# Buffers, order and slots of a two-block transformer kernel: six weight buffers, four row buffers, two late output units

## The chip, the cores and the metric

The kernel runs on one core of a Trainium2 chip. The metric is the device time of one execution in microseconds; the time before is 3179.68 us, the median of three runs (3179.25 to 3179.78).

## The reference

The input x has 256 tokens of width 2048, all in float32. A first block mixes and then applies retrieved experts; a second block has two layers. What matters here:

```python
# first block: attention (MLA and Fox heads, gated), then experts
x = x + jnp.einsum('bse,ed->bsd', merged, w_out[layer])
h2 = rms_norm(x, ffn_norm_g[layer])
...
# experts of one token: 8 heads, 16 experts each, out of 128 x 128
s1, i1 = lax.top_k(scores[:, :, 0], PEER_TOPK)
s2, i2 = lax.top_k(scores[:, :, 1], PEER_TOPK)
top_scores, top_pos = lax.top_k(cand_scores, PEER_TOPK)
experts = jnp.take_along_axis(cand_idx, top_pos, axis=-1)
...
a = jnp.einsum('td,thkd->thk', xb, u[eb])          # 128 rows of u for each token
w = gates * jax.nn.gelu(a, approximate=False)
x = x + jnp.einsum('thk,thkd->td', w, v[eb])       # 128 rows of v for each token
# second block, twice:
proj = x @ w_in
y = jnp.concatenate([ya, yb, yc], axis=-1) @ w_out # attentions and a convolution
x = layer_norm(ALPHA * x + y, ln_g, ln_b)
```

## The kernel before

The tokens are two tiles t = 0, 1 of 128, one token to a partition. There are eight passes in this order (PASSES): layer1(0), experts(0), layer1(1), experts(1), then layer2(l, t) as (0, 0), (1, 0), (0, 1), (1, 1). In layer 2 the run number is r = 2t + l + 1, so the last two passes are r = 3 and r = 4; tile 1 needs keys and values of tile 0 only.

Weights. All weight matrices are cut into units of 128 x 2048 floats, 1 MB. STREAM lists the units of all passes in the order in which PE uses them; each is 4 matmuls of 128x512, shown in the trace as 8 instructions. SP goes through FETCHES and loads them into a ring of RING = 4 slots; it waits until PE has used the unit that had the slot. Some units go two by two in one transfer of 2 MB (PAIRED, from a given row of a pass on), which needs both slots free. On PE, `unit()` waits for the arrival. `units` (L1445) multiplies with the normalised input, `out_units` (L1481) and `fin_units` (L1489) sum the output product in the four banks of psO; the last four units of a pass, "fin", each finish one bank.

Expert rows. For each tile POOL gathers 128 rows of u and 128 of v for every token: one `gather(n)` (L1001) brings one row of 2048 floats to each of 128 partitions, 1 MB, n = 0 to 511. They land in NB = 6 buffers `rows` and, in some ranges of n, one more in `hrow`. `allowed(n)` says which buffers a gather may use: the last one holds the work space of the top-k selection of tile 0 until that is over. DVE takes row after row in `slot()`: a dot product (L398) for u, a multiply-add into x (L405) for v. `row_used` lets POOL reuse the buffer.

Who does what when is written out by hand. `stage(m)` gives DVE m rows to work through during a stage, and `mix(f)` makes it go up to the fraction f of them at that place; EMIX, MIX1 and MIX2 hold the numbers. So DVE's rows for tile 0 lie in experts(0), layer1(1) and experts(1), those for tile 1 in experts(1), layer2(0, 0) and layer2(1, 0). SP starts to fetch for layer2(0, 1) when all but four rows are used, and that pass begins when all are.

The selection in `experts(t)`: for each i of four, two heads, PE computes queries (units), transposes them (`keys_T`) and multiplies with the sub-keys (`scores`, L1758). DVE copies the scores (L749), takes the 16 best twice (`top16`) and writes expert numbers to `eid`; `ids_ready` then lets POOL gather. In the order before, PE has one unit of the next chunk ahead of keys_T and one ahead of scores.

In layer 2, r = 2 leaves its sums in psO; DVE takes them at the start of r = 3 (`add_out(0, 0.0)`, L567), and with ACT's squares (`layer_squares`) makes the statistics (`layer_end`); `apply_ln(0)` in r = 3 writes the result of tile 0, and POOL stores it between its two convolutions. Between r = 3 and r = 4, layer_end gives the normalised x of tile 1 (L948, `xh_ready`), which PE transposes in `x_first` (L1457).

The fetch loop and the rule for pairs:

```python
_two = _u % 2 == 0 and _u + 1 < len(STREAM) and STREAM[_u][0] in PAIRED and STREAM[_u + 1][0] == STREAM[_u][0] \
    and STREAM[_u][1] >= PAIRED[STREAM[_u][0]] and STREAM[_u][2] == STREAM[_u + 1][2] == UNIT
...
if (p, row) == (("b", 0, 1), 0):
    sp.wait_ge(row_used, 4 * SLOTS - 4)
```

## Time and profile before

| | |
|---|---|
| median of three runs | 3179.68 us |
| the profiled execution: its time, its span | 3179.64 us, 3177.5 us |
| PE busy | 2525.9 us, 79% |
| DVE busy | 1922.3 us, 60% |
| POOL busy | 1059.2 us, 33% |
| ACT busy | 532.5 us, 17% |
| DMA | 1193.54 MB, mean 376 GB/s |
| SP's queue (weights); POOL's queue (gathers) | 644.12 MB; 538.86 MB |
| chain that ended last | PE 41%, DMA 39%, DVE 9%, POOL 6% |
| mean granted TensorE clock | 0.898 of full |

PE's sequence of busy tenths in 40 slices begins with seven nines, falls to 5 to 8 in the middle, and ends with nines again; the DMA's is nine in nearly all slices. Times in the trace are microseconds from the start of the span. A row with [2.23 <-DMA ring<-in_w] says that the engine was idle 2.23 us before it and what released it. The queue of SP is SPq, and a row of it covers several issues merged. "PE psP" and the like name the tile that is written.

### The profile page before, as it was taken

The page shows a single profiled execution, that of the slowest core. Times are in us where ns is not written, and L with a number is a line of the kernel's source. Part 1 is how long each engine was busy: PE and PEld are TensorE (multiplying, and loading weights), DVE is VectorE, ACT ScalarE, POOL GpSimd, SP SyncE. Part 2 cuts the span into 40 slices and gives each one's busy share as a digit, 9 for nine tenths or more (in the row PEclk, how much of TensorE's full clock was granted, in tenths as well). Part 3 has the DMA queues.
Part 4 walks back from the last instruction along what each step waited for, and adds up shares of the span by engine and source line. Part 5 has one row for each costly group of instructions (what it writes and reads, how often), then busy time and mean ns, then how long its engine had stood idle before and what let it go on. Part 6 is the DMA issues. An engine that isn't in the chain of part 4 may idle for free.

```text
span 3177.5 us, 20533 instructions
## 1 busy us (share of the span) xinstructions
PE 2525.9 (79%) x6976; PEld 1226.4 (39%) x6976; DVE 1922.3 (60%) x2978; ACT 532.5 (17%) x1371; POOL 1059.2 (33%) x649
## 2 busy tenths in 40 slices
PE   9999999837667668585879676566886589999998
PEld 4444444413233234233435332222543234444443
DVE  1656544877576666666895656675676653452533
ACT  3222122111102101011104201011410011111111
POOL 0000000355363444543443445533553424400710
PEclk9999999968879878787999888788898799999999
DMA  9888888999999999999999999999999999988886
GB/s 341 293 305 293 291 288 304 421 421 424 424 420 424 424 417 425 423 416 420 418 424 394 423 424 424 423 421 424 424 421 425 423 369 323 314 303 269 282 290 230
DMA packets 152280, 1193.54 MB, mean 376 GB/s; under 512 B 16552, under 2 KB 20280, under 8 KB 23536
## 3 DMA queue, kind: packets, MB, share of 16 engines
q1 hardware_dynamic: 73184, 644.12, 53.8%
q0 software_dynamic: 74192, 538.86, 40.8%
q10 hardware_dynamic: 4800, 9.25, 0.8%
q8 instruction: 56, 0.92, 0.1%
q14 instruction: 48, 0.39, 0.0%
HBM read 1190.07 MB, written 2.10 MB: 375 GB/s over the span
## 4 chain that ended last, share of the span: by engine, by line
PE 41%; DMA 39%; DVE 9%; POOL 6%; issue 3%; ACT 1%; DVEq 0%; SPq 0%; ACTq 0%
PE psP L1445 29%; DMA rows<-in_peer_u,tk 16%; DMA rows<-in_peer_v,tk 15%; PE psO L1481 6%; POOL rows L1001 5%; DMA ring<-in_w 4%; DVE rows L398 3%; DMA hrow<-in_peer_v,tk 2%; DVE x_sb L405 2%; PE psO L1489 2%; DMA ring<-in_wq 1%; DMA hrow<-in_peer_u,tk 1%; PE psX L1557 1%; POOL hrow L1001 1%; PE psO L1803 1%
## 5 line engine op out<-in xcount | busy, mean ns | idle before, releaser
L1445 PE MATMUL psP<-ring,hT 128*128 128x512 f32 x3584 | 1661.6, 620 | 135.2 <-DMA ring<-in_w 125.9
L1445 PEld LDWEIGHTS psP<-ring,hT 128*128 128x128 f32 x3584 | 700.5, 200 | 1010.4 <-issue 893.2
L1001 POOL DMA_INDIRECT rows<-in_peer_u,tk x222 | 391.8, 1765 | 981.1 <-DVEq L770 525.3
L405 DVE SCALAR_TENSOR_TENSOR x_sb<-rows,tk,x_sb 128x2048 f32<-128x2048 f32 x223 | 524.3, 2351 | 232.0 <-DMA rows<-in_peer_v,tk 214.5
L398 DVE CUSTOM_DVE_ANT_0 rows<-rows,hrow 128x2048 f32<-128x2048 f32 x222 | 503.5, 2290 | 214.0 <-DMA rows<-in_peer_u,tk 210.1
L1001 POOL DMA_INDIRECT rows<-in_peer_v,tk x223 | 394.2, 1768 | 471.7 <-DVE x_sb L405 392.6
L1481 PE MATMUL psO<-ring,work 128*128 128x512 f32 x832 | 390.0, 623 | 38.3 <-issue 22.8
L422 DVE STREAM_TRANSPOSE work<-work 32x128 f32<-32x128 f32 (+2 forms) x864 | 271.1, 314 | 151.0 <-ACT work L1321 83.2
L1481 PEld LDWEIGHTS psO<-ring,work 128*128 128x128 f32 x832 | 164.4, 202 | 236.0 <-issue 227.6
L1595 PE MATMUL psX<-kst,work 128*128 128x128 f32 x68 | 16.5, 388 | 157.5 <-DVEq L547 145.5
L1445 PE MATMUL psP<-ring,work 128*128 128x512 f32 (+1 forms) x288 | 122.4, 579 | 24.0 <-DMA ring<-in_w 23.5
L1134 ACT ACTIVATE work<-work,small 128x256 f32<-128x256 f32 (+1 forms) x128 | 56.6, 443 | 424.3 <-DVEq L519 424.3
L405 DVE SCALAR_TENSOR_TENSOR x_sb<-hrow,tk,x_sb 128x2048 f32<-128x2048 f32 x33 | 77.6, 2351 | 44.9 <-DMA hrow<-in_peer_v,tk 42.3
L398 DVE CUSTOM_DVE_ANT_0 hrow<-hrow 128x2048 f32<-128x2048 f32 x34 | 77.8, 2290 | 42.2 <-DMA hrow<-in_peer_u,tk 41.5
L1001 POOL DMA_INDIRECT hrow<-in_peer_u,tk x34 | 65.9, 1939 | 101.3 <-DVE tk L398 78.6
L1489 PE MATMUL psO<-ring,work 128*128 128x512 f32 x192 | 89.1, 622 | 11.5 <-DMA ring<-in_w 10.1
L1445 PEld LDWEIGHTS psP<-ring,work 128*128 128x128 f32 x288 | 57.3, 202 | 85.0 <-issue 82.5
L1001 POOL DMA_INDIRECT hrow<-in_peer_v,tk x33 | 58.9, 1785 | 89.1 <-DVE x_sb L405 72.5
L1303 ACT ACTIVATE work<-kst,cols 128x128 f32<-128x128 f32 x248 | 76.1, 389 | 46.1 <-PE psO L1803 46.0
L1020 POOL TENSOR_TENSOR work<-work 128x512 f32<-128x512 f32 x60 | 76.2, 1271 | 4.7
L1595 PEld LDWEIGHTS psX<-kst,work 128*128 128x128 f32 x68 | 10.9, 194 | 169.7 <-DVEq L547 155.4
L1803 PE MATMUL psO<-work 128*128 128x128 f32 x496 | 63.7, 283 | 15.0 <-ACT work L1303 15.0
(368 smaller groups left out, 1649.6 us busy)
## 6 DMA issues: line engine op xcount, KB each, us to landing
ring<-in_w SPq DMA_DIRECT2D x332, 1024.0 KB, 5.4
ring<-in_w SPq DMA_DIRECT2D x120, 2048.0 KB, 11.6
ring<-in_wq SPq DMA_DIRECT2D x32, 1024.0 KB, 9.4
ring<-in_w SPq DMA_DIRECT2D x8, 512.0 KB, 5.9
rows<-in_peer_v,tk POOLq DMA_INDIRECT x223, 22.5
rows<-in_peer_u,tk POOLq DMA_INDIRECT x222, 21.1
rows<-in_gate_bias SPq DMA_DIRECT2D x1, 2048.0 KB, 12.5
work<-in_sub_keys ACTq DMA_DIRECT2D x2, 1024.0 KB, 8.0
```

The costliest lines, as they stand in the source:

```text
L398: V.tensor_tensor_reduce(out=row_buf(n), in0=row_buf(n), in1=hrow[:, t, :], scale=1.0, scalar=0.0, op0=ALU.mult, op1=ALU.add, accum_out=do ...
L405: V.scalar_tensor_tensor(out=x_sb[:, t, :], in0=row_buf(n), scalar=dots[t][:, k:k + 1], in1=x_sb[:, t, :], op0=ALU.mult, op1=ALU.add).then ...
L422: own.add(V.transpose(dst[b_:b_ + 32, :, a_:a_ + 32], src[a_:a_ + 32, :, b_:b_ + 32]))
L1001: pool.indirect_dma_start(out=row_buf(n), out_offset=None, in_=a["peer_u" if s < SLOTS else "peer_v"], in_offset=bass.IndirectOffsetOnAxis ...
L1020: own.link(T(cacc, cacc, csq, ALU.add))
L1134: ins = A(W4[:, j, :], W4[:, j, :], ACT.Exp, bias=negm[:, 4 * u + j:4 * u + j + 1], accum_out=lsum[:, 4 * u + j:4 * u + j + 1])
L1303: ins = A(diag[n % 2][:, c, :], ident, ACT.Copy, scale=col("conv_w", (l * CC + c) * TAPS + k))
L1445: last = MM(psP[:, c % 2, 0:wide], src[:, kk, :], w[:, k, :], start=(kk == 0 and not begun), stop=(kk == 4 * nu - 1))
L1481: last = MM(psO[:, d, :], src[:, k, :], w[:, d, :], start=(bool(first) and k == 0), stop=False)
L1489: last = MM(psO[:, d, :], src[:, k, :], w[:, k, :], start=False, stop=(k == 3))
L1557: last = MM(o, qT[:, j, :], kT[:, j, :], start=plain, stop=(plain or bank_ends))
L1803: last = MM(psO[:, 0, P * m:P * (m + 1)], diag[n % 2][:, m, :], convh[:, m, k:k + P], start=(k == 0 and m == 0), stop=(k == TAPS - 1 and m ...
```

## The change

- The ring has six slots instead of four; `rows` four buffers instead of six. The one further buffer in hrow stays. The last of the four is open from n = 16 (4 + the 12 rows planned in experts(0)) instead of the last of six from n = 15.
- experts(0): PE transposes the first queries and computes their scores before it goes on to the next chunk. DVE's selection is the function `choose(t, i, h0, h1)` for heads h0 to h1; for the first two heads it runs head by head, and after the first one `head_ready` opens gathers 0 to 15; gather 16 waits for the second head.
- Pairs: all units of layer1(1), layer2(0, 0) and layer2(1, 0) that make a pair in the packed weights go two by two, instead of from row 24 or 8 on.
- The rows in experts(0) are 0, 1, 3, 5, 3 in its five stages instead of 0, 0, 4, 5, 0, and 11 instead of 14 in the first stage of layer1(1). The fractions of layer2(0, 0) change from 0.35, 0.45, 0.6 to 0.6, 0.65, 0.8.
- Late units: of the four last units of layer2(1, 0) the third and fourth move behind layer2(0, 1). PE multiplies them (`late_unit`) at the start of layer2(1, 1), one before the first transposes of x and one after the second, into banks of psO that are free by then, from a copy of the left operand kept in `mT_late`. DVE takes the incomplete sums at the start of r = 3 (`take_sums`), and adds the late part and makes the statistics in r = 4 (`add_late`, then layer_end). ACT's squares and apply_ln of tile 0 move to r = 4 too, and POOL stores tile 0 after both convolutions. The order of the statistics semaphores becomes TURN.

Left out of the diff: the two new semaphores' names in the lists, context lines, and the old selection, which is the same as choose for both heads.

```diff
@@ -24,7 +24,7 @@
...
 UNIT = 2048
-RING = 4
+RING = 6
 NEG = -1.0e30
...
@@ -34,7 +34,7 @@
...
 SLOTS = PH * TOPK
-NB = 6
+NB = 4
 N1 = 8
...
@@ -61,16 +61,19 @@
...
-EMIX = [[0, 0, 4, 5, 0], [10, 6, 6, 6, 0]]
-MIX1 = [14, 28, 21, 35, 21, 34, 20, 33, 25]
+EMIX = [[0, 1, 3, 5, 3], [10, 6, 6, 6, 0]]
+FIRST = TOPK
+MIX1 = [11, 28, 21, 35, 21, 34, 20, 33, 25]
 GELU1 = 4
 EARLY = 0.25
+LATE = 2
+TURN = {1: 1, 3: 2, 2: 3, 4: 4}
 MIX2 = [[20, 33, 63], [43, 32, 53]]
...
-    return list(range(NB - 1)) + ([NB - 1] if n >= 15 else []) + ([NB] if 24 <= n < 228 or n >= 256 else [])
+    return list(range(NB - 1)) + ([NB - 1] if n >= NB + sum(EMIX[0]) else []) + ([NB] if 24 <= n < 228 or n >= 256 else [])
...
@@ -125,15 +128,21 @@
...
     for _row, (_name, _g, _q) in enumerate(_order):
+        if _p == ("b", 1, 0) and _name == "fin" and _q >= LATE:
+            continue
         _kind = GROUPS[_g] if _p[0] == "a" else "n"
...
         STREAM.append((_p, _row, width(_name), _how, _ended[_how]))
-
-
-PAIRED = {("a", 1): 24, ("b", 0, 0): 8, ("b", 1, 0): 8}
+    if _p == ("b", 0, 1):
+        for _d in range(LATE, 4):
+            _ended["bank"] += 1
+            STREAM.append((("b", 1, 0), len(_order) - 4 + _d, UNIT, "bank", _ended["bank"]))
+
+
+PAIRED = {("a", 1): 0, ("b", 0, 0): 0, ("b", 1, 0): 0}
 ODD = {_p: [_u for _u, _s in enumerate(STREAM) if _s[0] == _p][0] % 2 for _p in PAIRED}
...
@@ -141,7 +150,7 @@
...
     _two = _u % 2 == 0 and _u + 1 < len(STREAM) and STREAM[_u][0] in PAIRED and STREAM[_u + 1][0] == STREAM[_u][0] \
-        and STREAM[_u][1] >= PAIRED[STREAM[_u][0]] and STREAM[_u][2] == STREAM[_u + 1][2] == UNIT
+        and STREAM[_u][1] >= PAIRED[STREAM[_u][0]] and (STREAM[_u][1] + ODD[STREAM[_u][0]]) % 2 == 0 and STREAM[_u + 1][1] == STREAM[_u][1] + 1 and STREAM[_u][2] == STREAM[_u + 1][2] == UNIT
     FETCHES.append((_u, 2 if _two else 1))
...
@@ -283,6 +292,7 @@
...
         mTc = qT
+        mT_late = v3(wk(768, 1280), P)
         diag = [csq, cacc]
...
@@ -295,7 +305,7 @@
...
         lnc = v3(kv[:, 2048:2304], P)
-        lnc_far = v3(rows[:, 4, 0:256], P)
+        lnc_far = v3(hrow[:, 0, 0:256], P)
...
@@ -574,6 +584,28 @@
...
+            def take_sums():
+
+                for d in range(4):
+                    if d < LATE:
+                        seen["bank"] += 1
+                    dve.wait_ge(bank_done, seen["bank"])
+                    V.tensor_copy(x_sb[:, 0, 512 * d:512 * (d + 1)], psO[:, d, :]).then_inc(x_added, 1)
+
+            def add_late():
+
+                for d in range(LATE, 4):
+                    seen["bank"] += 1
+                    dve.wait_ge(bank_done, seen["bank"])
+                    xv = x_sb[:, 0, 512 * d:512 * (d + 1)]
+                    V.tensor_tensor(xv, xv, psO[:, d - LATE, :], ALU.add).then_inc(late_added, 1)
+                dve.wait_ge(late_added, 4 - LATE)
+                dve.wait_ge(x_added, 16)
+                link(V.tensor_reduce(msum, v3(x_sb[:, 0, :], 512), AX, ALU.add))
+                link(V.tensor_reduce(part3[:, 0:1], msum[:, 0:3], AX, ALU.add))
+                link(V.tensor_scalar(shift[:, 0:1], part3[:, 0:1], -1.0 / 1536, None, ALU.mult))
+                dve.sem_inc(ln_part, 1)
+
             def turn_P(t):
...
@@ -588,12 +620,12 @@
...
                 link(V.tensor_scalar(dev, dev, -1.0, 1e-5, ALU.mult, ALU.add))
-                dve.wait_ge(sq_done, r)
+                dve.wait_ge(sq_done, TURN[r])
                 link(V.scalar_tensor_tensor(out=bias, in0=ssl[:, 0:1], scalar=1.0 / D, in1=dev, op0=ALU.mult, op1=ALU.add))
...
             def layer_rs(t, r):
-                dve.wait_ge(sd_ready, r)
+                dve.wait_ge(sd_ready, TURN[r])
                 link(V.reciprocal(rsl[:, t:t + 1], vart[:, 2:3]))
...
@@ -742,31 +774,43 @@
...
                 idx3 = v3(idxu, TOPK)
+
+                def choose(t, i, h0, h1):
+
+                    m, heads, ways, picks = h1 - h0, slice(256 * h0, 256 * h1), slice(32 * h0, 32 * h1), slice(16 * h0, 16 * h1)
+                    top16([(sc[:, j, :], vals[:, j, :], idx3[:, j, :]) for j in range(2 * h0, 2 * h1)])
+                    own.add(V.tensor_copy(idxf[:, ways], idxu[:, ways]))
+                    v4_ = vals[:, 2 * h0:2 * h1, :].rearrange("p (h c) k -> p h c k", c=2)
+                    d4 = idxf[:, ways].rearrange("p (h c k) -> p h c k", c=2, k=TOPK)
+                    c4 = cand[:, heads].rearrange("p (h a b) -> p h a b", a=TOPK, b=TOPK)
+                    e4 = eq[:, heads].rearrange("p (h k j) -> p h k j", k=TOPK, j=TOPK)
+                    link(V.tensor_tensor(c4, v4_[:, :, 0, :].unsqueeze(3).to_broadcast([P, m, TOPK, TOPK]),
+                                         v4_[:, :, 1, :].unsqueeze(2).to_broadcast([P, m, TOPK, TOPK]), ALU.add))
+                    best = gates[t][:, 32 * i:32 * (i + 1)]
+                    top16([(cand[:, 256 * h:256 * (h + 1)], best[:, 16 * h:16 * (h + 1)], posu[:, 16 * h:16 * (h + 1)])
+                           for h in range(h0, h1)])
+                    for c, (op, amount) in enumerate(((ALU.logical_shift_right, 4), (ALU.bitwise_and, 15))):
+                        link(V.tensor_scalar(posh[:, picks], posu[:, picks], amount, None, op))
+                        link(V.tensor_copy(posx[:, picks], posh[:, picks]))
+                        link(V.tensor_tensor(v3(eq[:, heads], TOPK), rep(posx[:, picks], TOPK), over(iota, 16 * m), ALU.is_equal))
+                        link(V.tensor_tensor(e4, e4, d4[:, :, c, :].unsqueeze(2).to_broadcast([P, m, TOPK, TOPK]), ALU.mult))
+                        link(V.tensor_reduce((p0, p1)[c][:, picks], v3(eq[:, heads], TOPK), AX, ALU.add))
+                    link(V.scalar_tensor_tensor(out=posx[:, picks], in0=p0[:, picks], scalar=float(NK), in1=p1[:, picks],
+                                                op0=ALU.mult, op1=ALU.add))
+                    link(V.tensor_copy(eid[t][:, 32 * i + 16 * h0:32 * i + 16 * h1], posx[:, picks]))
+
                 for i in range(4):
...
                     dve.sem_inc(sc_taken, 1)
...
+                    if t == 0 and i == 0:
+                        choose(t, i, 0, 1)
+                        dve.sem_inc(head_ready, 1)
+                        choose(t, i, 1, 2)
+                    else:
+                        choose(t, i, 0, 2)
                     dve.sem_inc(ids_ready, 1)
...
@@ -814,20 +858,22 @@
...
                 stage(MIX2[l][0] if t == 0 else 0)
-                early, last = (EARLY, 0.35, 0.45, 0.6) if l == 0 else (0.3, 0.83, 0.87, 0.92), (1.0, 1.1)[l]
+                early, last = (EARLY, 0.6, 0.65, 0.8) if l == 0 else (0.3, 0.83, 0.87, 0.92), (1.0, 1.1)[l]
                 if l == 0:
...
                 if r == 3:
-                    add_out(0, 0.0)
-                    layer_end(1, 0, 2)
+                    take_sums()
                     link(V.tensor_scalar(x_sb[:, 1, :], x_sb[:, 1, :], ALPHA, None, ALU.mult))
...
                 if r == 4:
+                    dve.wait_ge(lnrow_in, 64)
                     link(V.scalar_tensor_tensor(out=x_sb[:, 1, :], in0=x_sb[:, 1, :], scalar=ALPHA, in1=ln_g0, op0=ALU.mult, op1=ALU.mult))
                     link(V.scalar_tensor_tensor(out=x_sb[:, 1, :], in0=ln_b0, scalar=ALPHA, in1=x_sb[:, 1, :], op0=ALU.mult, op1=ALU.add))
+                    add_late()
+                    layer_end(1, 0, 2)
                 mix(early[0])
...
@@ -914,7 +960,7 @@
...
                         mix(1.0)
-                if l == 0 and t == 1:
+                if l == 1 and t == 1:
                     apply_ln(0)
...
@@ -990,9 +1036,11 @@
...
                 k, b = s % SLOTS, BUF[n]
-                if s < SLOTS and s % 32 == 0:
+                if s < SLOTS and (s % 32 == 0 and n or n == FIRST):
                     pool.wait_ge(ids_ready, 4 * t + s // 32 + 1)
-                if n == 15:
+                if n == 0:
+                    pool.wait_ge(head_ready, 1)
+                if BUF[n] == NB - 1 and NB - 1 not in BUF[:n]:
                     pool.wait_ge(ids_ready, 4)
...
@@ -1031,9 +1079,8 @@
...
                     conv(l, 1, step)
-                if l == 0:
-                    pool.wait_ge(x_norm, 4)
-                    pool.dma_start(out[:, 0, :], x_sb[:, 0, :]).then_inc(out0_sem, 16)
+            pool.wait_ge(x_norm, 4)
+            pool.dma_start(out[:, 0, :], x_sb[:, 0, :]).then_inc(out0_sem, 16)
             pool.wait_ge(out0_sem, 16)
...
@@ -1306,7 +1353,7 @@
...
                 take_xT(split, "copy" if l == 0 else "ln")
-                if l == 0 and t == 1:
+                if l == 1 and t == 1:
                     layer_squares(0, 2)
...
@@ -1379,7 +1426,7 @@
...
                 if t == 0:
-                    take_mT(mTc)
+                    take_mT(mT_late if l else mTc)
                 if r != 2:
...
@@ -1390,13 +1437,16 @@
...
                 own.link(A(vart[:, 3:4], kc("one"), ACT.Sqrt))
-                act.wait_ge(ln_part, r)
+                act.wait_ge(ln_part, TURN[r])
+                if r == 2:
+                    act.wait_ge(late_added, 4 - LATE)
                 own.add(A(junk[:, 0:1536], x_sb[:, t, 0:1536], ACT.Square, bias=shift[:, t:t + 1], accum_out=ssl[:, 0:1]))
...
                 act.sem_inc(sq_done, 1)
-                act.wait_ge(x_added, 8 + 4 * r)
+                if r != 2:
+                    act.wait_ge(x_added, 8 + 4 * r)
                 own.link(A(junk[:, 1536:2048], x_sb[:, t, 1536:2048], ACT.Square, bias=shift[:, t:t + 1], accum_out=ssl[:, 1:2]))
-                act.wait_ge(var_ready, r)
+                act.wait_ge(var_ready, TURN[r])
                 A(vart[:, 2:3], ssl[:, 1:2], ACT.Sqrt, scale=1.0 / D, bias=vart[:, 0:1]).then_inc(sd_ready, 1)
...
@@ -1446,7 +1496,7 @@
...
-            def x_first(split, src, ready, key, between=None):
+            def x_first(split, src, ready, key, between=None, head=None, mid=None):
...
@@ -1460,8 +1510,12 @@
...
+                if head is not None:
+                    head()
                 turn(0)
                 turn(1)
+                if mid is not None:
+                    mid()
                 c = begin(key)
...
@@ -1471,19 +1525,27 @@
...
-            def out_units(k0, k1, src, first, last_group=False):
+            def out_units(k0, k1, src, first, ends=4):
...
                     for d in range(4):
-                        last = MM(psO[:, d, :], src[:, k, :], w[:, d, :], start=(bool(first) and k == 0), stop=False)
+                        last = MM(psO[:, d, :], src[:, k, :], w[:, d, :], start=(bool(first) and k == 0), stop=(k == 3 and d >= ends))
                     last.then_inc(unit_used, 1)
-            def fin_units(src):
+            def late_unit(d):
+
+                pe.wait_ge(x_added, 16 + d - LATE + 1)
+                w = v3(unit(), 512)
+                for k in range(4):
+                    last = MM(psO[:, d - LATE, :], mT_late[:, k, :], w[:, k, :], start=(k == 0), stop=(k == 3))
+                last.then_inc(bank_done, 1)
+
+            def fin_units(src, upto=4):
                 pe.wait_ge(mT_ready, n_["mT"])
-                for d in range(4):
+                for d in range(upto):
                     w = v3(unit(), 512)
...
@@ -1762,6 +1824,11 @@
...
                     c = begin(("e", t, "pq", i))
+                    if t == 0 and i == 1:
+                        keys_T(0)
+                        scores(0)
+                        units(c, 0, 4, 4, hT)
+                        continue
                     units(c, 0, 1, 4, hT)
...
@@ -1783,7 +1850,8 @@
...
                 else:
-                    x_first(split, x_sb[:, t, :], lambda r_: pe.wait_ge(xh_ready, 4 * t + r_ + 1), ("b", l, t, "u", 0))
+                    x_first(split, x_sb[:, t, :], lambda r_: pe.wait_ge(xh_ready, 4 * t + r_ + 1), ("b", l, t, "u", 0), None,
+                            (lambda: late_unit(LATE)) if t else None, (lambda: late_unit(LATE + 1)) if t else None)
...
@@ -1815,6 +1883,8 @@
...
                     pe.wait_ge(x_added, before)
+                    if r == 4:
+                        pe.wait_ge(late_added, 4 - LATE)
                     pe.wait_ge(sc_taken, 8)
...
@@ -1911,8 +1981,8 @@
...
                 e_move()
-                out_units(2, 4, mT, None)
-                fin_units(mTc)
+                out_units(2, 4, mT, None, LATE if r == 2 else 4)
+                fin_units(mT_late if r == 2 else mTc, LATE if r == 2 else 4)
...
```

## Rows read from the trace of the kernel before

**Rows 1.** Windows, whole span: us; busy us by engine (instructions); TensorE clock; DMA share; GB/s.
```profile
0.00:545.00 545.00, 535.21 (x1460) 255.49 (x1461) 273.47 (x897) 138.94 (x366) 5.58 (x12) 1.00 0.88 300
545.00:2590.00 2045.00, 1417.97 (x3998) 702.08 (x3997) 1406.71 (x1494) 309.43 (x830) 908.87 (x510) 0.85 1.01 421
2590.00:3178.00 588.00, 572.73 (x1520) 268.83 (x1520) 242.09 (x589) 84.14 (x175) 144.74 (x127) 0.98 0.84 287
```

**Rows 2.** Timeline, start, SP and PE: start, us, engine, line, op, count [idle before].
```profile
29.38 0.43 SPq L1064 DMA_DIRECT2D rows<-in_gate_bias  x1
31.97 41.53 SPq L1061 DMA_DIRECT2D ring<-in_w  x12
...
44.56 13.97 PE L1445 MATMUL psP<-ring,hT 128*128 128x512 f32 x32 [2.23 <-DMA ring<-in_w]
```

**Rows 3.** DMA issues from 100 to 500 us: count, KB each, median us to landing.
```profile
ring<-in_w SPq DMA_DIRECT2D x106, 1024.0 KB, 5.3
```

**Rows 4.** Timeline, first expert pass: PE scores, DVE's copy of them, POOL's first gather.
```profile
524.16 1.05 PE L1758 MATMUL psO<-work 128*128 128x128 f32 x8
...
525.33 0.69 DVE L749 COPY rows<-psO 128x512 f32<-128x512 f32 x1 [14.80 <-PE psO L1758]
...
542.63 1.04 POOL L1001 DMA_INDIRECT rows<-in_peer_u,tk  x1 [525.35 <-DVEq L770]
```

**Rows 5.** Windows just before and just after the first gather.
```profile
505.00:542.00 37.00, 37.00 (x108) 17.96 (x108) 19.58 (x70) 12.30 (x18) 0.00 (x0) 1.00 0.78 266
...
550.00:560.00 10.00, 10.00 (x34) 5.17 (x33) 9.25 (x28) 0.60 (x1) 0.00 (x0) 1.00 1.01 427
```

**Rows 6.** DMA issues from 545 to 2590 us; then POOL's issues in the timeline.
```profile
ring<-in_w SPq DMA_DIRECT2D x120, 2048.0 KB, 11.6
...
rows<-in_peer_u,tk POOLq DMA_INDIRECT x220, 21.3
...
647.49 0.94 POOL L1001 DMA_INDIRECT rows<-in_peer_u,tk  x1 [4.04 <-DVE tk L398]
...
655.87 3.03 POOL L1001 DMA_INDIRECT rows<-in_peer_u,tk  x1 [2.47 <-DVE tk L398]
```

**Rows 7.** The page's groups: DVE's dot product with one gathered row.
```profile
L398 DVE CUSTOM_DVE_ANT_0 rows<-rows,hrow 128x2048 f32<-128x2048 f32 x222 | 503.5, 2290 | 214.0 <-DMA rows<-in_peer_u,tk 210.1
```

**Rows 8.** Waits from 1660 to 1700 us (total, times, longest); a window there.
```profile
DVE kv L533 <- PE psX L1514: 20.6, 1, 20.6
...
1690.00:1710.00 20.00, 20.00 (x91) 12.71 (x90) 11.35 (x18) 10.48 (x40) 7.01 (x5) 0.95 0.80 307
```

**Rows 9.** Timeline, end of the middle stage: SP's fetches, last rows, last units.
```profile
2581.37 30.20 SPq L1061 DMA_DIRECT2D ring<-in_w  x7
2583.56 2.35 DVE L405 SCALAR_TENSOR_TENSOR x_sb<-rows,tk,x_sb 128x2048 f32<-128x2048 f32 x1 [1.34 <-DMA rows<-in_peer_v,tk]
2590.00 8.67 PE L1489 MATMUL psO<-ring,work 128*128 128x512 f32 x16 [5.28 <-DMA ring<-in_w]
2590.35 2.35 DVE L405 SCALAR_TENSOR_TENSOR x_sb<-rows,tk,x_sb 128x2048 f32<-128x2048 f32 x1 [4.43 <-DMA rows<-in_peer_v,tk]
2595.29 2.35 DVE L405 SCALAR_TENSOR_TENSOR x_sb<-rows,tk,x_sb 128x2048 f32<-128x2048 f32 x1 [2.60 <-DMA rows<-in_peer_v,tk]
2598.51 1.04 PE L1457 MATMUL psX<-kst,x_sb 128*128 128x128 f32 x8
```

**Rows 10.** Timeline of PE and one window at the start of the last pass.
```profile
2865.55 13.90 PE L1489 MATMUL psO<-ring,work 128*128 128x512 f32 x32
...
2882.59 1.42 PE L1457 MATMUL psX<-kst,x_sb 128*128 128x128 f32 x8 [3.15 <-DVE x_sb L948]
...
2885.77 5.75 PE L1445 MATMUL psP<-ring,hT 128*128 128x512 f32 x8
...
2880.00:2890.00 10.00, 6.52 (x17) 3.58 (x18) 4.46 (x16) 4.12 (x11) 0.00 (x0) 0.66 0.34 116
```

**Rows 11.** Timeline, DVE's first work after apply_ln in the third pass.
```profile
2838.39 1.13 DVE L544 SCALAR_TENSOR_TENSOR work<-psX,small,work 128x128 f32<-128x128 f32 x4 [11.11 <-PE psX L1585]
```

27 lines of the change are left out of this document (4 added, 23 removed).

## Prediction

> **What bounds the kernel now.** The windows come first, because the busy shares of the whole span mix three stages. Up to 545 us PE is busy 535.21 of 545 us at a granted clock of 1.00 while the DMA moves 300 GB/s; from 545 to 2590 us the DMA share is 1.01 and it moves 421 GB/s, and PE is busy only 1418 of 2045 us at 0.85; after 2590 PE is bound again, 572.73 of 588 us [rows 1]. So stage 1 ends when PE has done its units, stage 2 when its bytes have come in, and stage 3 when PE has done the rest. In stage 2 a wait of PE or DVE costs nothing as long as some transfer is queued. There only three things can move the end: bytes fetched before stage 2 begins, bytes taken out of it, and its rate. A unit or a gathered row is 1.05 MB, 2.5 us at 421 GB/s.
>
> The profiled execution took 3179.64 us (span 3177.5, 2.1 around it); the median of three is 3179.68. I count changes of the span and subtract them from 3179.7.
>
> **Six ring buffers at the start.** The first nine ring fetches are issued one by one as slots come free, then x (tile 1) and the gate bias, 3 MB together, and only at 31.97 the tenth unit; PE waits 2.23 us for it at 44.56 [rows 2]. With six slots the tenth fetch is issued two units earlier (7 us: 32 matmuls of 13.97 us are four units), with the same 3 MB ahead of it. Gain between 0 and 2.23; the DMA is nearly full from 10 to 40 us, but it has some room before that. I take the whole: **-2.2**.
>
> **Six ring buffers at the border of stages 1 and 2.** In stage 1 the DMA has 29% to spare, and a unit lands 5.3 us after its issue [rows 3], so that the ring is full ahead of PE. With two more slots two more units (2.1 MB) are in when stage 2 begins. All of them are needed before stage 2 ends, so the gain is 2 x 2.5 us: **-5.0** (bounds 0 and -5.0; 0 if the deeper ring only shifts the balance to the rows' cost, which is case B below).
>
> **First row numbers by one head.** Before, PE transposes the first queries after one unit of the next chunk and computes scores after another (the scores' matmuls run at 524.16); DVE takes them at 525.33 and POOL issues the first gather at 542.63 [rows 4]. The new order has no unit between, which saves about 4 us to the scores (two units are 7, less an estimated 3 for ACT's two copies, which PE now sees bare). From the copy to the gather are 17.3 us, 16.6 without the copy, for two heads; one head has half the instructions in the top-16 steps and half the width in the others, but the fixed part of each small one stays: I take 9.9. So the first gather goes out at about 532, 11 us earlier. Until then the DMA moves 266 GB/s (505 to 542), and just after it 427 [rows 5]; nearer the usual 300 of stage 1 the spare is about 125 GB/s, so 11 us bring 1.4 MB, **-3.3** (bounds: -1.5 if three row buffers fill too soon, -4.5 with 427 against 266). Three buffers are 3.1 MB, and at that spare rate they last the 11 us. The second head costs DVE some 3 us more in all; DVE isn't what stage 2 waits for. The row plan moves three rows ahead of the pass (12 instead of 9) and takes 3 out of its first stage, sum nil. In the 5-row burst after the third selection only three rows can be at hand; DVE waits some 8 us there, covered by the ring, which still owes PE units. If that cover is gone, it is 8 us of half-used DMA, 4 us.
>
> **Slots placed anew.** Row buffers become 4 plus one in hrow instead of 6 plus one; with the ring the sum in flight stays 11 MB. Gathers land 21.3 us after their issue [rows 6], mostly queueing. What a row buffer needs without queueing: a unit's 5.3 us as the nearest row for landing, 0.93 to 3.03 for the issue on POOL, and 2.29 on DVE [rows 3, 6, 7], so 8.5 to 10.6 us; five buffers at full rate take 5 x 2.5 = 12.5 us per turn. So five rows alone still keep the DMA full, with little to spare. From gather 228 to 255 hrow is closed, and four buffers have only 10 us per turn; there the ring must help. I charge **+2** for longer dry stretches (bounds 0 and case B).
>
> The Trainium skill, SBUF — State Buffer, "Who interferes with whom", says that GpSimd and DVE share a port pair, and that POOL is held back while certain DVE instructions run. It speaks against fewer row buffers. Without it the turn of a buffer would be the 8.5 us and the charge nil; with it every gather may slip by a DVE instruction, the turn is 10.6, and the charge is the +2. The trace agrees: 0.93 us for an issue with DVE idle, 3.03 with DVE in its row loop.
>
> **The dip at 1690.** In the first pass over tile 0 in layer 2's part, DVE waits 20.6 us for PE's keys, the row buffers are all full, and the ring of two pairs has one pair in flight: 307 GB/s from 1690 to 1710 [rows 8] against 421 over the stage. That is 2.3 MB, 5.4 us. Now three pairs leave two in flight while PE uses the third, and the mix fractions (0.35, 0.45, 0.6 become 0.6, 0.65, 0.8) put 5 more of the 20 rows ahead of that wait. Fewer row buffers act against it. I take 0.7 of it: **-3.8** (0 to -5.4).
>
> **All pairs in the middle part.** 24 + 8 + 8 units of these passes now come two by two. A pair lands in 11.6 us [rows 6]. That is 181 GB/s, no more than a half of the DMA, and the total rate of 421 is that of a stage with both kinds: **-0.5** (0 to -1).
>
> **Two late output units.** They leave stage 2: 2.1 MB, at most -5.0. But look at its end. At 2581.37 four rows are left and SP may fetch for the next pass; PE waits 5.28 us for the last pair, uses it to 2598.5, and the last row is added from 2595.29 [rows 9]. Both end together. The gate for SP (four rows left) is unchanged, and now up to six free slots are filled at once with first units of the next pass, which share the DMA with the last rows just as the last pair did. Only what of the pair had moved before the gate is gained, about one unit, **-2.5**; the rest is early bytes for a stage that doesn't need them. Bounds 0 and -5.0.
>
> The Trainium skill, DMA: Bandwidth & Descriptors, "Queues, rings and completion order", says that each DMA engine takes turns between its queues, a packet at a time. A pair has runs of 16 KB and single units and rows 8 KB, so by that rule the last rows, which now share with single units, would get a half instead of a third; over the 12 us of the pair that is 2 us more, and the term would be -4.5. The trace leans that way: 6.8 us between the additions of two rows while the last pair is in flight (2583.56, 2590.35) and 4.9 beside single units (2590.35, 2595.29).
>
> In stage 3 the two units go into the change from layer 0 to layer 1 of tile 1. There PE is idle 3.15 us for the normalised x, then again for ACT's copies, and its clock drops to 0.66 of full, so that the first unit (8 matmuls) takes 5.75 us [rows 10] instead of 3.5. From the end of the output product (2865.55 + 13.90 = 2879.5) to the end of that unit are 12.1 us. Afterwards: three units at 3.5 (13.90 for four) and transposes of 1.1 and 0.6, 12.1 to 12.6 us with the clock at full. So 7 us of matmuls cost **+0.3** (bounds -0.5 and +3.5, if the second of them isn't hidden).
>
> DVE gets add_late, the statistics and apply_ln of tile 0 in the last pass. The first lie before the u chunk's copy is needed, with the 14 us of PE's next chunk between (four units). apply_ln is eight instructions on a quarter of a row's width, by 2.29 us for a row 4.6 us and something for the start of each; it sits at the same place of the pass as before, where DVE is idle 11.11 us behind it [rows 11]. Behind the waits of ACT's squares stands only its u copy. The write of out, tile 0, follows the last convolution on POOL, some 80 us before the end, and hides. All **0**.
>
> **Sum.** -2.2 - 5.0 - 3.3 + 2.0 - 3.8 - 0.5 - 2.5 + 0.3 = -15.0: 3179.7 - 15.0 = **3164.7**.
>
> **The rivals.** (A) Only the head start counts: the deeper ring and the early gathers bring 8.3 us, the dip stays because five row buffers are full sooner, the end isn't sooner by the late units, the start doesn't gain; with +2 this is 3173.4. For it: the end of stage 2 is balanced, and gains on one side alone do nothing there.
>
> (B) Slower: five row buffers run dry. Whenever DVE is away from rows (eight selections of 17 us each, waits up to 20.6 us) the rows' queue is empty two buffers sooner; if ring and rows are both stopped by each other, the DMA stands. The end of stage 2 moves by 2045 us times the loss in rate, and the 15 us are gone once 421 becomes 418. A mean of 416 costs 24.6 us: 3189. Against it: buffers in all are as many as before, and PE's and DVE's waits in stage 2 are mostly for the DMA.
>
> (C) Every term at its best: -2.2 - 5.0 - 4.5 - 5.4 - 1 - 5 - 0.5 and no charge for five buffers is -23.6: 3156.
>
> **How the numbers follow.** Forecast 0.55, A 0.20, B 0.10, C 0.15. The range reaches from below C to between A and B: 3152 to 3181. A measurement of this kernel can tell about 0.2%, 6.4 us, from no change: under 3173.3 lie the forecast, C and half of A: faster 0.80; same 0.11; slower 0.09.
>
> **What will show it.** First gather near 532 us, and the DMA above 420 GB/s from there; no PE wait at 42 to 44 us; 1690 to 1710 above 380 GB/s; the middle windows at 421 or more; the last row near 2584; PE without a gap between the output product and layer 1, clock 1.00. The prediction is wrong if the middle rate falls below 419, if the last rows take more than the 16 us they take now from SP's gate on, or if the last pass of stage 3 has new PE waits.

## The result: slower, 3246.9 us

Median of five runs 3246.89 us (3243.76 to 3249.51) against 3179.78; the ratio is 1.0206, 95% interval 1.0195 to 1.0216. The forecast was 3164.7, the range ended at 3181. The profiled execution took 3244.26 us, its span 3242.5.

The windows of the kernel after, in the first two stretches of [rows 1]:

```profile
core 0: us, PE busy (x) PEld busy (x) DVE busy (x) ACT busy (x) POOL busy (x), PEclk, DMA share, GB/s
0.00:545.00 545.00, 535.23 (x1461) 255.28 (x1462) 279.90 (x920) 138.94 (x366) 7.42 (x14) 1.00 0.89 307
545.00:2590.00 2045.00, 1309.56 (x3916) 665.50 (x3914) 1353.80 (x1458) 307.38 (x826) 843.40 (x490) 0.81 0.98 405
```

Stage 1 moves 307 GB/s where it moved 300: 545 us x 7 GB/s = 3.8 MB more are in when stage 2 begins. Stage 2 moves 405 where it moved 421, which is 3.8% of 2045 us, 78 us. PE is busy 1310 us of it, not 1418, and DVE 1354, not 1407: both wait longer. The border of stages 2 and 3 has moved by 64 us, from 2598.51 [rows 9] to 2662.55, and stage 3 lasts 580.0 us after, 579.0 before. The whole loss lies in stage 2. The timeline at its end:

```profile
2648.73 20.88 SPq L1108 DMA_DIRECT2D ring<-in_w  x7
2660.08 2.35 DVE L415 SCALAR_TENSOR_TENSOR x_sb<-hrow,tk,x_sb 128x2048 f32<-128x2048 f32 x1 [2.62 <-DMA hrow<-in_peer_v,tk]
2662.55 2.56 PE L1507 MATMUL psX<-kst,x_sb 128*128 128x128 f32 x12 [4.57 <-DVEq L837]
```

The page's part 2, in 40 slices of 81 us, the kernel after (the DMA's share in tenths, then GB/s):

```profile
DMA  9888888999999999999998999999999999989886
GB/s 377 299 301 285 299 285 323 379 394 390 422 397 411 408 408 413 419 394 405 421 385 352 424 417 422 409 393 425 410 417 414 419 389 326 320 283 300 280 290 219
```

There is no one place: of the slices 8 to 32, which are stage 2, 14 move less than 412 GB/s, and they are spread over all of it. In windows of 5 us from 545 to 2590 (409 of them) the DMA share is under 0.90 in 25, before in 2. The mean share fell from 1.009 to 0.984 (2.5%, 51 us in which DMA engines stood), and the GB/s for a full share from 417 to 412 (1.3%, 26 us). Together these two are the 78 us, within rounding. The 3.8 MB of the head start and the 2.1 MB of the two late units are 14 us less to move at 421 GB/s, and 78 less 14 is the 64 us by which the border moved.

### The profile page after: what moved, and what is told of

It reads as the page before. It is cut to its first block, busy times and chain, and to the rows that moved or that the text cites. A ratio compares the mean times of both kernels' runs of the same rounds, so it can differ in the third digit from the quotient of the medians.

```text
span 3242.5 us, 20545 instructions
## 1 busy us (share of the span) xinstructions
PE 2450.5 (76%) x6976; PEld 1205.1 (37%) x6976; DVE 1926.6 (59%) x2991; ACT 531.3 (16%) x1370; POOL 1034.3 (32%) x649
## 4 chain that ended last, share of the span: by engine, by line
PE 38%; DMA 34%; DVE 16%; POOL 7%; issue 4%; ACT 1%; DVEq 0%; SPq 0%; ACTq 0%; POOLq 0%
PE psP L1495 26%; DMA rows<-in_peer_v,tk 13%; DMA rows<-in_peer_u,tk 12%; PE psO L1535 6%; POOL rows L1049 6%; DVE x_sb L415 4%; DMA hrow<-in_peer_v,tk 4%; DMA hrow<-in_peer_u,tk 4%; DVE rows L408 4%; PE psO L1551 1%; PE psO L1871 1%; POOL hrow L1049 1%; DVE hrow L408 1%; PE psX L1619 1%; DMA ring<-in_w 1%
## 5 line engine op out<-in xcount | busy, mean ns | idle before, releaser
L1495 PE MATMUL psP<-ring,hT 128*128 128x512 f32 x3584 | 1607.9, 605 | 4.7 <-DMA ring<-in_wq 2.3
L1495 PEld LDWEIGHTS psP<-ring,hT 128*128 128x128 f32 x3584 | 687.2, 195 | 839.4 <-issue 828.1
L1049 POOL DMA_INDIRECT rows<-in_peer_u,tk x209 | 350.6, 1678 | 1026.9 <-DVEq L810 511.7
L415 DVE SCALAR_TENSOR_TENSOR x_sb<-rows,tk,x_sb 128x2048 f32<-128x2048 f32 x210 | 493.7, 2351 | 268.5 <-DMA rows<-in_peer_v,tk 252.9
L408 DVE CUSTOM_DVE_ANT_0 rows<-rows,hrow 128x2048 f32<-128x2048 f32 x209 | 475.3, 2290 | 264.9 <-DMA rows<-in_peer_u,tk 261.2
L1049 POOL DMA_INDIRECT rows<-in_peer_v,tk x210 | 364.8, 1737 | 515.5 <-DVE x_sb L415 448.4
L1535 PE MATMUL psO<-ring,work 128*128 128x512 f32 x832 | 380.9, 612 | 32.7 <-issue 32.7
L408 DVE CUSTOM_DVE_ANT_0 hrow<-hrow 128x2048 f32<-128x2048 f32 x47 | 107.7, 2291 | 60.0 <-DMA hrow<-in_peer_u,tk 58.3
L415 DVE SCALAR_TENSOR_TENSOR x_sb<-hrow,tk,x_sb 128x2048 f32<-128x2048 f32 x46 | 108.2, 2352 | 52.9 <-DMA hrow<-in_peer_v,tk 48.8
L1049 POOL DMA_INDIRECT hrow<-in_peer_u,tk x47 | 85.6, 1822 | 109.8 <-DVE tk L408 101.2
L1049 POOL DMA_INDIRECT hrow<-in_peer_v,tk x46 | 85.0, 1847 | 93.9 <-DVE x_sb L415 76.5
L1495 PE MATMUL psP<-ring,work 128*128 128x512 f32 (+1 forms) x288 | 113.5, 545 | 0.4 <-ACT work L1290 0.4
L1551 PE MATMUL psO<-ring,work 128*128 128x512 f32 x176 | 79.2, 609 | 1.4 <-ACT work L1194 1.4
L1495 PEld LDWEIGHTS psP<-ring,work 128*128 128x128 f32 x288 | 54.0, 190 | 55.6 <-issue 53.1
```

Of the source, the lines that this page charges most:

```text
L408: V.tensor_tensor_reduce(out=row_buf(n), in0=row_buf(n), in1=hrow[:, t, :], scale=1.0, scalar=0.0, op0=ALU.mult, op1=ALU.add, accum_out=do ...
L415: V.scalar_tensor_tensor(out=x_sb[:, t, :], in0=row_buf(n), scalar=dots[t][:, k:k + 1], in1=x_sb[:, t, :], op0=ALU.mult, op1=ALU.add).then ...
L1049: pool.indirect_dma_start(out=row_buf(n), out_offset=None, in_=a["peer_u" if s < SLOTS else "peer_v"], in_offset=bass.IndirectOffsetOnAxis ...
L1495: last = MM(psP[:, c % 2, 0:wide], src[:, kk, :], w[:, k, :], start=(kk == 0 and not begun), stop=(kk == 4 * nu - 1))
L1535: last = MM(psO[:, d, :], src[:, k, :], w[:, d, :], start=(bool(first) and k == 0), stop=(k == 3 and d >= ends))
L1551: last = MM(psO[:, d, :], src[:, k, :], w[:, k, :], start=False, stop=(k == 3))
```

## Where the DMA stands, in the trace

The timeline of the kernel after from 1688 to 1728 us: SP's row, some of POOL and DVE, and PE's. The columns are start, duration, engine and line, and in brackets the idle time before and who ended it:

```profile
1688.68 0.33 SPq L1106 DMA_DIRECT2D ring<-in_w  x1
...
1698.35 0.94 POOL L1049 DMA_INDIRECT rows<-in_peer_u,tk  x1 [6.46 <-DVE tk L408]
1698.83 0.87 DVE L736 MAX8 kv<-kv 128x8 f32<-128x128 f32 x4
1714.79 0.18 DVE L800 CAST tk<-kv 128x32 uint32<-128x32 f32 x1
1715.80 2.29 DVE L408 CUSTOM_DVE_ANT_0 rows<-rows,hrow 128x2048 f32<-128x2048 f32 x1 [0.19 <-DVE tk L820]
1718.37 2.75 POOL L1049 DMA_INDIRECT rows<-in_peer_u,tk  x1 [19.08 <-DVE tk L408]
...
1727.61 1.12 PE L1948 MATMUL psX<-kst,work 128*128 128x128 f32 x4 [39.31 <-DVE work L879]
```

and the windows of the same stretch:

```profile
1700.00:1705.00 5.00, 0.00 (x0) 0.00 (x0) 4.83 (x29) 0.00 (x0) 0.00 (x0) 0.50 0.99 415
1705.00:1710.00 5.00, 0.00 (x0) 0.00 (x0) 4.75 (x19) 0.00 (x0) 0.00 (x0) 0.50 1.01 419
1710.00:1715.00 5.00, 0.00 (x0) 0.00 (x0) 4.66 (x10) 0.00 (x0) 0.00 (x0) 0.50 0.25 103
1715.00:1720.00 5.00, 0.00 (x0) 0.00 (x0) 4.67 (x5) 0.31 (x1) 1.63 (x1) 0.50 0.00 0
1720.00:1725.00 5.00, 0.00 (x0) 0.00 (x0) 5.00 (x7) 0.00 (x0) 4.39 (x3) 0.50 0.63 215
```

DVE leaves the rows at 1698 for the last selection of tile 1 and is back at 1715.80. The last gather before it goes out at 1698.35, the next at 1718.37: POOL sat idle 19.08 us for a row buffer. Five buffers hold 5 x 2.5 = 12.5 us of transfers, to 1711. From there the DMA moves 103 GB/s, then 0. The ring can't help: PE waits 39.31 us for a product of DVE's (L879) that is queued behind the selection and a burst of rows, all six slots have landed, and SP asks for nothing after 1688.68. Rows and ring stand because of the same engine, so their bytes in flight don't add up. This is the largest hole of the stage.

The common form is shorter. DVE serves a burst of rows, then one step of attention:

```profile
937.22 3.75 PE L1603 MATMUL psX<-work,kst 16*128 16x512 f32 x4 [16.06 <-DVE work L706]
940.39 0.94 POOL L1049 DMA_INDIRECT hrow<-in_peer_u,tk  x1 [0.31 <-issue]
944.72 1.66 DVE L513 SCALAR_TENSOR_TENSOR work<-psX,small,kst 128x256 f32<-128x256 f32 x4 [5.44 <-PE psX L1619]
947.82 2.29 DVE L408 CUSTOM_DVE_ANT_0 rows<-rows,hrow 128x2048 f32<-128x2048 f32 x1 [0.19 <-DVE small L528]
948.95 0.33 SPq L1106 DMA_DIRECT2D ring<-in_w  x1
950.39 2.75 POOL L1049 DMA_INDIRECT rows<-in_peer_u,tk  x1 [9.05 <-DVE tk L408]
```

PE waited 16.06 us for DVE's L706 (the ring filled meanwhile), then DVE waits 5.44 us for PE and does its products; POOL waits 9.05 us, SP fetches again at 948.95. The same step in the kernel before:

```profile
919.42 3.75 PE L1541 MATMUL psX<-work,kst 16*128 16x512 f32 x4 [16.18 <-DVE work L674]
926.91 1.66 DVE L503 SCALAR_TENSOR_TENSOR work<-psX,small,kst 128x256 f32<-128x256 f32 x4 [5.43 <-PE psX L1557]
932.58 2.75 POOL L1001 DMA_INDIRECT rows<-in_peer_u,tk  x1 [9.05 <-DVE tk L398]
```

and the windows, two of the kernel before and then one of the kernel after:

```profile
925.00:930.00 5.00, 5.00 (x16) 3.15 (x16) 2.88 (x5) 0.08 (x1) 0.00 (x0) 0.76 1.01 423
930.00:935.00 5.00, 5.00 (x13) 2.28 (x12) 4.99 (x5) 2.00 (x8) 2.42 (x1) 1.00 1.03 406
```

```profile
945.00:950.00 5.00, 5.00 (x11) 2.05 (x10) 4.78 (x6) 2.08 (x8) 0.00 (x0) 0.89 0.51 184
```

The waits are the same to 0.2 us, and SP is silent in both (before, it fetches nothing from 889 to 930.72; after, nothing from 907 to 948.95). With both rings silent the row buffers make the difference: seven carry the DMA through, five leave it at a share of 0.51.

DVE is away from the rows for 8.6 us here, less than the 12.5 us that five buffers hold, and still the DMA runs dry. The reason is the rest of a buffer's turn: the row's own use by DVE, the issue and the landing come on top, which the prediction put at 8.5 to 10.6 us. 8.6 plus that is 17.1 to 19.2 us (an estimate from rows), over 12.5 and close to the 17.5 of seven. Longer absences can pass without harm if the ring asks meanwhile. In the kernel after, before the gather of 1602.03, POOL stands for a whole selection, but SP sends fetches at 1584.68 and 1592.91:

```profile
1602.03 3.00 POOL L1049 DMA_INDIRECT rows<-in_peer_v,tk  x1 [18.51 <-DVE x_sb L415]
...
1585.00:1600.00 15.00, 12.70 (x38) 5.92 (x37) 14.05 (x52) 0.93 (x2) 0.00 (x0) 1.00 1.02 427
```

The 25 windows under 0.90 lack 43 of the 51 us. About 20 of the 43 lie behind four of the selections, the rest behind absences of 9 us at most. Up to gather 15, at 640.62, only three row buffers are open in the kernel after and five in the kernel before, so the holes up to there come from fewer buffers still.

That five buffers carry the rows in steady work, as the prediction worked out, is true, and it isn't the question:

```profile
2250.00:2300.00 50.00, 0.00 (x0) 0.00 (x0) 45.30 (x20) 0.00 (x0) 38.77 (x18) 0.50 1.01 420
```

Here DVE does nothing but rows and PE nothing at all: 420 GB/s.

The waits of stage 2 (545 to 2600; total, times, longest), the kernel after, and under it two of the lines with ring 4 and four row buffers (e2):

```profile
POOL rows L1049 <- DVE tk L408: 491.2, 89, 19.1
PE psX L1657 <- DVEq L557: 311.6, 11, 36.3
DVE rows L408 <- DMA rows<-in_peer_u,tk: 261.2, 116, 8.5
```

```profile
DVE rows L408 <- DMA rows<-in_peer_u,tk: 255.9, 124, 6.4
PE psX L1657 <- DVEq L557: 164.4, 11, 22.3
```

With the deep ring PE runs ahead until it waits for DVE, 311.6 us at this line where the kernel with a ring of 4 has 164.4, and a ring in front of a waiting PE fills up and asks for nothing. Depth isn't all of it: with a ring of 4 and single fetches (e12 below) the line has 263.7 us.

## Experiments

Kernels marked * are built on the changed kernel. "Under 0.90" counts the windows of 5 us as above; "border" is the start of the first transposes of the last pass.

| kernel | ring / rows | what else | median us | ratio to before | border | GB/s 545-2590 | under 0.90 |
|---|---|---|---|---|---|---|---|
| before | 4 / 6 | | 3179.8 | 1 | 2598.5 | 421 | 2 |
| after | 6 / 4 | | 3246.9 | 1.0206 [1.0195, 1.0216] | 2662.6 | 405 | 25 |
| e1* | 4 / 6 | | 3177.7 | 0.9988 [0.9978, 0.9998] | 2595.0 | 421 | 4 |
| e2* | 4 / 4 | | 3234.8 | 1.0171 [1.0144, 1.0199] | 2655.6 | 408 | 25 |
| e3 | 6 / 4 | on before | 3244.0 | 1.0196 [1.0179, 1.0213] | 2662.9 | 407 | 18 |
| e4* | 5 / 5 | | 3194.0 | 1.0039 [1.0025, 1.0053] | 2611.9 | 416 | 12 |
| e5* | 6 / 4 | no pairs | 3222.5 | 1.0154 [1.0116, 1.0192] | 2642.2 | 409 | 15 |
| e6* | 6 / 4 | selections split | 3236.7 | 1.0175 [1.0159, 1.0190] | 2655.2 | 406 | 24 |
| e7* | 4 / 6 | pairs as before | 3175.8 | 0.9983 [0.9974, 0.9992] | 2593.8 | 421 | 2 |
| e8* | 4 / 6 | e7 + row plan | 3172.8 | 0.9975 [0.9965, 0.9984] | 2590.4 | 422 | 2 |
| e9* | 4 / 6 | e8, no late units | 3177.9 | 0.9990 [0.9981, 0.9999] | 2598.6 | 422 | 3 |
| e10* | 4 / 6 | e8, no first head | 3175.6 | 0.9980 [0.9971, 0.9989] | 2594.6 | 422 | 1 |
| e11* | 4 / 6 | e8, gate at 2 | **3167.8** | 0.9960 [0.9947, 0.9974] | 2585.3 | 421 | 2 |
| e12* | 4 / 4 | no pairs | 3231.4 | 1.0150 [1.0135, 1.0166] | 2649.2 | 409 | 16 |
| e13* | 3 / 7 | e11 | 3244.6 | 1.0195 [1.0178, 1.0213] | 2659.6 | 411 | 17 |
| e14* | 4 / 6 | e11, mixes as before | 3172.9 | 0.9975 [0.9965, 0.9986] | 2589.9 | 421 | 3 |
| e15* | 4 / 6 | e11, no pairs | 3177.9 | 0.9992 [0.9983, 1.0001] | 2598.5 | 420 | 1 |
| e16* | 6 / 4 | e5 + e6 + gate | 3214.9 | 1.0106 [1.0091, 1.0122] | 2633.9 | 410 | 15 |
| e17* | 4 / 6 | e8, gate at 0 | 3172.3 | 0.9974 [0.9965, 0.9983] | 2585.8 | 420 | 4 |

The ratios are taken against the runs of the kernel before made beside each kernel. Kernels with four row buffers have four or five runs each, and two of them scatter: e2 took from 3229.3 to 3246.6 us, and of e5 three runs took 3218.8 to 3222.7 and one 3248.7. A difference of 10 us that involves these two is not resolved.

### Which part costs it: e1 to e4

Theory R says that the loss comes from the fewer row buffers, Rival O from everything but the slots, Rival Q from the deeper ring, whose fetches take turns of the DMA from the rows.

```diff
 # e1                # e2                # e4                # e3, on before
-RING = 6            -RING = 6           -RING = 6           -RING = 4
+RING = 4            +RING = 4           +RING = 5           +RING = 6
-NB = 4                                  -NB = 4             -NB = 6
+NB = 6                                  +NB = 5             +NB = 4
```

e3 also moves lnc_far from rows to hrow, as the change does; e4 fetches a pair only where its slots lie side by side in a ring of 5.

> The changed kernel with the old buffers: ring of 4, row buffers 6; all else of the change stays. Theory R (too few row buffers: the ring fills, stands still, and five rows don't carry the DMA through DVE's other work): the middle stage is full again, 3160 to 3182 us. Rival O (the new order, the pairs, the late units or the first head cost it): 3230 to 3250.

> The changed kernel with a ring of 4 and 4 row buffers: two ring slots taken away, nothing given back. Theory R (only the row buffers count in the middle stage, the two further slots hold weights that PE can't use yet): 3240 to 3265 us, no more than 20 us above the changed kernel. Rival Q (the deeper ring takes DMA turns from the rows): faster than the changed kernel, 3190 to 3225. If buffers count alike wherever they are: 3290 or more.

> The kernel before with a ring of 6 and 4 row buffers, nothing else. Theory R: the loss is here already, 3235 to 3265 us. Rival O: 3170 to 3185.

> The changed kernel with a ring of 5 and 5 row buffers (a unit whose pair would wrap around the ring comes alone). Theory R: about half of the loss, 3195 to 3225 us, or less than half if the loss is steeper at the last buffer. Rival O: 3240 to 3250.

Measured: with the slots put back, all the rest of the change is 4 us faster than before (e1), no case for Rival O. The slots alone, on the kernel before, make 3244.0 (e3). From 6 row buffers to 4 at a ring of 4 are 57 us (e1 to e2); from a ring of 4 to one of 6 are another 12 (e2 to after), about what e2's runs scatter, which R leaves open and Q would explain. e2 lies 5 us under the range that R gave, and above that of Q. 5 and 5 lie between, at +12 on before and 1 us under R's range: the loss is steeper at the last buffer. Theory R holds for the larger part.

### Two halves of the mechanism: e5 and e6

```diff
 # e5
-PAIRED = {("a", 1): 0, ("b", 0, 0): 0, ("b", 1, 0): 0}
+PAIRED = {("a", 1): 999, ("b", 0, 0): 999, ("b", 1, 0): 999}
 # e6
-                        choose(t, i, 0, 2)
+                        choose(t, i, 0, 1)
+                        mix(0.5)
+                        choose(t, i, 1, 2)
```

> The changed kernel (ring of 6, 4 row buffers) with every ring fetch a single unit, no pairs at all. Theory R says that the DMA stands while DVE is away from the rows, because the row buffers are full and the ring is full too; with pairs a freed slot asks for nothing until its neighbour is free as well. If this second half of the mechanism is real, single fetches shorten the dry stretches and take back 5 to 20 us of the 67: 3227 to 3242, and the row buffers stay the main cause. If the pairs have no part in it: 3247, within 3. If single fetches are worse in themselves (8 KB runs beside rows): over 3250. Rival Q (the deeper ring takes turns from the rows) expects less here than R, since a single unit takes a smaller share beside a row: below 3225.

> The changed kernel with each selection after the first of tile 0 done head by head, with up to half a stage's rows between the two heads: DVE is away from the rows for about 10 us at a time and not for 17. Five row buffers hold 12.5 us at 421 GB/s. Theory R (buffers run full while DVE is away) expects a gain here, though head by head costs DVE some 3 us more per selection: 3215 to 3240, with fewer stretches below 350 GB/s between 550 and 1000 us. If DVE's absences aren't what makes the DMA stand: 3247 to 3270, the added DVE time alone.

Split selections take back 10 us, inside R's range: they shorten DVE's absences, but only at six selections. The last of tile 1 has no rows planned for its stage, so nothing comes between its heads, and the largest hole stays (10 and 25 GB/s from 1705 to 1715). Windows like those at 735 and 945, where DVE does steps of attention, stay too (24 under 0.90). Single fetches take back 24 by the medians, 2 us into Q's range, and 17 by the ratios, inside R's; e12 was made to tell the two apart. The reason by R is the grain of the ring: a slot that comes free asks at once, where a pair waits for its neighbour. e5's windows under 0.90 fall to 15 and the mean share rises to 0.997, but its rate for a full share is only 411 GB/s against 412 for the kernel after.

### The rest of the change: e7 to e11, e14, e17

```diff
 # e7: e1 with
+PAIRED = {("a", 1): 24, ("b", 0, 0): 8, ("b", 1, 0): 8}
 # e8: e7 with
+EMIX = [[0, 2, 4, 5, 0], [10, 6, 6, 6, 0]]
+MIX1 = [12, 28, 21, 35, 21, 34, 20, 33, 25]
 # e9: e8 with
+LATE = 4
 # e11: e8 with (e17: 4 * SLOTS)
-                    sp.wait_ge(row_used, 4 * SLOTS - 4)
+                    sp.wait_ge(row_used, 4 * SLOTS - 2)
 # e14: e11 with
+                early, last = (EARLY, 0.35, 0.45, 0.6) if l == 0 else (0.3, 0.83, 0.87, 0.92), (1.0, 1.1)[l]
 # e10: e8 with
-                        choose(t, i, 0, 1)
-                        dve.sem_inc(head_ready, 1)
-                        choose(t, i, 1, 2)
+                        choose(t, i, 0, 2)
```

In e9 the two calls of late_unit in x_first go as well, in e10 gather 0 waits for ids_ready.

> The changed kernel with ring of 4 and 6 row buffers (3177.7 when run before) and with pairs only from row 24, 8 and 8 of the three passes, as in the kernel before. In that run 550 to 600 us had 373 GB/s against 422 before, with one pair in flight in a ring of 4: 50 x (1 - 373/421) = 5.7 us. If the early pairs are the cause: 3172. If that dip comes from the new row plan, or if what is lost there is bounded elsewhere: 3177, within 2.

> As the run before it (ring of 4, 6 row buffers, pairs from 24, 8, 8) and the row plan of the first pass placed for six buffers: 0, 2, 4, 5, 0 rows in its stages and 12 in the next, in place of 0, 1, 3, 5, 3 and 11. With the early gathers (13 us earlier) and one row more taken early, the row buffers are emptied sooner and more gathers fit before 600 us: 3168 to 3172. If row buffers are never full between 530 and 600 us: as the run before it, within 2.

Both came out between or just beside what was expected. Pairs in the early part cost 1.9 us in a ring of 4 (e1 to e7), the row plan made for four buffers 2.9 (e7 to e8); the intervals of neighbours overlap, so that neither is shown by itself; the step from e1 to e8 is 5. From 550 to 600 us e1 moves 373 GB/s and e8 412.

> e8_pair_emix with no late output units: all four units of the output's last part stay in the middle part (LATE = 4), and x_first of the last pass has none between its transposes. The prediction gave the late units -2.5 in stage 2 and +0.3 in stage 3, so undoing them gives 3172.8 + 2.2 = 3175. If all 2.1 MB count as bytes taken out of a stage bound by the DMA, 3172.8 + 5 = 3178. In e8 PE waits 9.34 us for the last rows before the last pass; if the rows set that end by themselves (their buffers' turn, not the bytes), the two units cost nothing there and the time is 3172 to 3173.

> e8_pair_emix with the first selection of tile 0 done for both heads at once again, and gather 0 waiting for all of it; the scores still come without a unit between. The prediction put the first gather 11 us earlier, of which 4 by the scores and 7 by one head, at 125 GB/s of spare rate: -3.3 for all, about -2.1 for the part undone here: 3175. If the early gathers only fill buffers that then stand full, no change: 3173.

> e8_pair_emix with SP's gate before the first fetch of the pass after the rows at two rows left and not four. In e8 the four fetches at 2576.6 share the DMA with the last four rows, which are added at 2579.2, 2583.0 and 2587.9, and PE waits 9.34 us for them. If the last rows set the end, they come some 3 us sooner and the ring's first units still land in time: 3170. If the first units are then what PE waits for (10 us for four at 421 GB/s): 3172.8 to 3176.

Late units undone: +5.0, all of their 2.1 MB. First head undone: +2.8 in the medians, 1.6 by the ratios, with the intervals overlapping; from 500 to 550 us e10 moves 282 GB/s where e8 moves 305, 1.15 MB or 2.7 us, which agrees. The gate at two rows left: -5.0, more than the 3 expected (4.8 by the ratios, with the intervals of e8 and e11 overlapping; the timelines show the step too). The end of stage 2 in e8, then in e11:

```profile
2576.64 32.79 SPq L1108 DMA_DIRECT2D ring<-in_w  x8
2587.94 2.35 DVE L415 SCALAR_TENSOR_TENSOR x_sb<-rows,tk,x_sb 128x2048 f32<-128x2048 f32 x1 [2.62 <-DMA rows<-in_peer_v,tk]
2590.40 2.94 PE L1507 MATMUL psX<-kst,x_sb 128*128 128x128 f32 x12 [9.34 <-DVEq L837]
```

```profile
2577.84 7.30 DVE L415 SCALAR_TENSOR_TENSOR x_sb<-rows,tk,x_sb 128x2048 f32<-128x2048 f32 x3
2580.22 29.58 SPq L1108 DMA_DIRECT2D ring<-in_w  x10
2585.25 2.94 PE L1507 MATMUL psX<-kst,x_sb 128*128 128x128 f32 x12 [5.56 <-DVEq L837]
2587.98 3.85 PE L1495 MATMUL psP<-ring,hT 128*128 128x512 f32 x8
```

In e8 SP's next fetches go out at 2576.64 and the last three rows come 3.7 and 5.0 us apart. In e11 the last three stand ready and are added in a run of 7.30 us; the border is at 2585.25 and the first unit of the new pass is there at 2587.98.

> e11_gate with SP's gate behind the last row (none left) and not at two left. The last rows then have the DMA to themselves. If sharing still delays them, the end of stage 2 comes 1 to 2 us sooner, but the first unit lands only a unit's time after it: PE's transposes take 3 us and the unit alone some 3 to 5 us, so that the gain is spent: 3167 to 3171. If the cover matters more than the sharing: over 3171.

3172.3, the second case: 4.5 us slower than e11. The border is at 2585.75 and in e11 at 2585.25, so nothing was left of the sharing. But the first units come late: PE waits 2.52 us for the first and then takes 5.40 us for its 8 matmuls, 3.85 in e11:

```profile
2585.67 22.03 SPq L1108 DMA_DIRECT2D ring<-in_w  x8
2585.75 2.93 PE L1507 MATMUL psX<-kst,x_sb 128*128 128x128 f32 x12 [5.56 <-DVEq L837]
2591.20 5.40 PE L1495 MATMUL psP<-ring,hT 128*128 128x512 f32 x8 [2.52 <-DMA ring<-in_w]
```

> e11_gate with the mix fractions of the first pass of layer 2 as in the kernel before: 0.35, 0.45, 0.6 in place of 0.6, 0.65, 0.8. If the five rows moved ahead of the keys' work are what removed the dip at 1690 (307 GB/s for 20 us, 5.4 us), it comes back: 3167.8 + 4 to 5 = 3172 to 3173. If the dip went by the other row plan, 3168.

+5.1, and the dip is back: 306 and 333 GB/s from 1690 to 1710, 419 and 420 in e11. The mix fractions removed it with six row buffers.

```profile
1690.00:1700.00 10.00, 10.00 (x41) 5.96 (x40) 3.39 (x3) 4.10 (x16) 1.61 (x2) 0.93 0.75 306
1700.00:1710.00 10.00, 10.00 (x53) 6.89 (x53) 7.89 (x16) 6.32 (x24) 5.59 (x3) 1.00 0.90 333
```

### Pairs, depth and the other direction: e12, e13, e15, e16

```diff
 # e12: the changed kernel with RING = 4, NB = 4 and PAIRED all 999;  e15: e11 with PAIRED all 999
 # e13: e11 with (and pairs only where the two slots lie side by side)
+RING = 3
+NB = 7
 # e16: the changed kernel with the edits of e5, e6 and e11
```

> The changed kernel with ring of 4, 4 row buffers and single fetches throughout. Known: ring 6 in pairs 3246.9, ring 4 in pairs 3234.8, ring 6 in singles 3222.5. If a ring of pairs is worse only by its grain (a freed slot asks for nothing until its neighbour is free), then singles help a ring of 4 more than a ring of 6, for there a pair is half of it: below 3222. If the depth of the ring matters by itself the other way (Rival Q: more ring transfers in flight leave the rows less of the DMA), 3210 to 3222, about 12 under the ring of 6. If the depth helps once the grain is gone, as bytes in flight while DVE is away: 3225 to 3240.

Singles at 4 / 4: 3231.4, the third case. By the medians the deeper ring is worth 9 us in singles (e5), where by Q the shorter one should have won, but by the ratios the two are equal (1.0154 and 1.0150), so this doesn't decide. The traces say more. DVE's waits for gathered rows from 545 to 2600 add up to 591.5 us in e5 and 590.5 in e12: in singles the two further slots took nothing from the rows. In pairs they are 606.1 in the kernel after and 585.6 in e2, so there Q can have a part in the 12 us; that stays open.

> e11_gate with single fetches throughout, no pairs. With 4 row buffers singles were worth 24 us (ring 6) and 3 us (ring 4), by shorter dry stretches (25 of 409 windows of 5 us below a share of 0.90 in the changed kernel, 15 with singles), though the full DMA moved less (420 GB/s against 422 to 425). Here there are no dry stretches to shorten (2 of 409), so only the lower rate is left: 2045 us x 4/424 = 19 us at most, 10 as the middle: 3172 to 3187. If the grain counts here too: 3165.

Where rows have their buffers, single fetches cost 10 us: no dry stretches are left to shorten (1 window), and the rate for a full share is 415 GB/s against 417. That is inside the expected range.

> e11_gate with a ring of 3 and 7 row buffers (one more slot moved from the ring to the rows; a pair is fetched only where its two slots lie side by side, slots 0 and 1). Theory: DVE's absences are 17 us at most, 6 + 1 row buffers hold 17.5 us at 421 GB/s and cover them, so an eighth buffer finds nothing to cover, while PE with a ring of 3 waits for its units in stages 1 and 3: 3170 to 3185, slower than e11's 3167.8. Rival (rows are starved still, more buffers pay on): 3155 to 3165.

Worse by 77 us than e11, the first case's sign and far over its range. In stage 2 (545 to 2600) PE now waits for the ring 444 us at L1495, against 147 us at the same line (L1445) in the kernel before:

```profile
PE psP L1495 <- DMA ring<-in_w: 444.0, 106, 8.6
...
DVE kv L543 <- PE psX L1576: 42.8, 3, 35.6
```

DVE waits for PE behind it, once for 35.6 us, and is away from the rows for longer than eight buffers hold (20 us). Stage 1 is slower too: 293 GB/s, PE 527.58 us busy of 545 instead of 533.32 in e11. Whether an eighth row buffer beside a ring of 4 would help wasn't tried.

> The changed kernel (ring 6, 4 row buffers) with all remedies found: single fetches (-24.4), selections head by head (-10.2) and the gate at two rows left (-5). If they add up: 3207. If singles and split heads cover the same dry stretches: 3215 to 3220. In both cases above the 3180 of the kernel before, since waits of DVE for PE (attention's keys and scores) are longer than five row buffers cover; below 3185 would mean that row buffers aren't needed once the rest is mended.

3214.9, at the edge of the second case: the remedies overlap, and 35 us over the kernel before stay. Of all that was tried only row buffers took them back.

## Why the prediction was wrong, point by point

**The step that failed** is "Slots placed anew": +2, with "the sum in flight stays 11 MB" and a turn of 8.5 to 10.6 us against the 12.5 us of five buffers. It measured 69 us (e1 to after). There are three faults in it. It compared a turn in steady work with the buffers' time, and in steady work it is right (2250 to 2300 us above). The time that DVE is away has to be added to the turn, and it stood among the rows of the prediction: a selection of 17 us, a wait of 20.6 [rows 8]. An absence of 8.6 us was enough for five buffers to run dry and not for seven (945 and 925 us above); the absences of 17 us are longer than either stock covers with its turn, and pass only where the ring has something to fetch. It added ring and rows to one sum; but a ring slot asks for a transfer when PE moves on and a row buffer when DVE does, and both stop when PE waits for DVE. And it charged the fewer buffers and credited the pairs apart, while a pair delays the ring's request just when the rows are out (e5, with the reserve said there).

**Case B** named this mechanism, its condition and its formula, and got 0.10 and 416 GB/s. The rate was 405, so the loss in rate was three times what B priced. Its "against" was the sum in flight and the observation that PE's and DVE's waits in stage 2 were mostly for the DMA. For PE that was misread: its waits in the kernel before, from 545 to 2590, add up to 314 us for DVE and 177 for the DMA. In the kernel after they are 585 and 4. For DVE it is true, but with six buffers; it says nothing on four.

The other terms, each from the run that undoes it or from the trace:

- **Start, -2.2.** Right: PE waits 0.49 us and not 2.23 for the tenth unit, at 42.01.

```profile
42.01 13.97 PE L1495 MATMUL psP<-ring,hT 128*128 128x512 f32 x32 [0.49 <-DMA ring<-in_w]
```

- **Ring at the border, -5.0.** Right in size: with the start's it is 3.8 MB more by 545 us, of which the early gathers are 0.5 (e1 moves 301 GB/s there), so 3.3 MB, 7.8 us against the 7.2 forecast. The rates are rounded to 1 GB/s, which is 1.3 us here. No run got it without its price.
- **First row numbers, -3.3.** Near: the first gather is at 529.12 (forecast 532), 13.5 us sooner than before and not 11, because the scores come 7.5 us sooner (516.64) where 4 were forecast. The one head is worth 2.8 by the medians and 1.6 by the ratios (e10), where its part of the forecast was 2.1; no run undid the whole term.

```profile
529.12 1.04 POOL L1049 DMA_INDIRECT rows<-in_peer_u,tk  x1 [511.71 <-DVEq L810]
```

- **The dip, -3.8.** Right by the fractions: 5.1 from e11 to e14. The sign that the prediction named, over 380 GB/s from 1690 to 1710, came true by luck (423): the kernel after is at another place of the program by then, just ahead of the hole at 1710. Its copy of the keys (L543) comes at 1750.70, without a wait, and the DMA is full from there on. But PE had stood for 39 us shortly before, so this is no clean test of the term.

```profile
1750.00:1780.00 30.00, 28.46 (x117) 17.92 (x118) 25.82 (x31) 14.96 (x50) 14.96 (x9) 0.86 1.01 416
```

- **All pairs, -0.5.** Probably the wrong sign: +1.9 with six row buffers (e7), inside the noise, but with 373 GB/s against 392 from 550 to 600 us. With four no run takes this term apart; e5 also undoes the pairs that the kernel before had.
- **Late units, -2.5 and +0.3.** The first is undersized: -5.0 for both together (e9). In the profiled executions the border comes 8.2 us sooner with them; why it is more than the 5.0 us of their bytes wasn't tried. About 2.5 us of it are lost again in the first transposes and the first unit of the pass: in e8 PE had stood for 9.34 us, its granted clock is 0.50 from 2590 to 2594, and the unit's 8 matmuls take 5.20 us; in e9 they take 3.60, at 1.00. The second term is right: from the end of the output product to the end of layer 1's first unit are 11.6 us in e8 and 11.9 in e9, and PE has no wait in it, as forecast. The prediction read sharing at the border as a given that eats half of the gain; e11 shows that it is a choice of the gate.

By the rule of the Trainium skill that was weighed there (DMA: Bandwidth & Descriptors, "Queues, rings and completion order": each DMA engine takes turns between its queues) the term would have been -4.5, and e9's 5.0 agrees better with that than with -2.5. It agrees in the number only; no run varied how the queues share.

- **Together** the terms other than ring and slots were -3.3 - 3.8 - 0.5 - 2.5 + 0.3 = -9.8; e8, which has these edits with a row plan and pairs for its own slots, is 7.2 us under before. These parts were sound, and were 7 us of a change whose slots cost 69.

**What beats both**: e11, 3167.8 us, ratio 0.9960 [0.9947, 0.9974], the changed kernel with ring 4, six row buffers, the old pairs, a row plan for them and the gate at two rows left.

**Open.** Why a ring of 6 in pairs is 12 us worse than a ring of 4 (if it is: e2's runs scatter by 17 us): the share is 0.984 against 0.987 (6 us) and the rate for a full share 412 against 414 (8 us), so it is both, but no run took either apart. And why the rate for a full share lies between 410 (singles, four row buffers) and 417 (before): its order by kernels is stable, its cause wasn't tried.

## What to carry to other kernels

Size the buffers of a stream by the turn of one buffer plus the time in which its consumer is away, not by the turn alone: bytes in flight on another queue don't stand in for them when both queues wait, directly or through each other, for the same engine. Before slots are moved from one stream to another, list for each the gaps between two of its consumer's steps, mark those in which the other stream asks for nothing, and compare gap plus turn with slots x time of one transfer; both directions can be wrong (e13 and after are equally slow). And gate the first transfers of the next stage by what the last ones of this stage need: two rows left was right here, four or none cost 4 to 5 us each.

## What the runs showed of the hardware that I had not expected

- Single fetches of 1 MB in place of pairs of 2 MB lower what the busy DMA engines move: 417 GB/s for a full share with pairs, 415 with singles at 4 / 6, and 414 against 410 at 4 / 4. Where nothing else is lost, e15 is 10 us slower than e11 with them.
- The granted clock of PE fell to 0.50, 1.2 GHz, while PE stood for 39 us (1700 to 1725), and to 0.81 on the mean of stage 2 where it was 0.85. What that costs in stage 2 wasn't tried: the DMA bounds the stage, but from 940 to 945 PE works at 0.50 on the product for which DVE waits 5.44 us, in the kernel before as well (0.50 from 920 to 925).
